# Leaving out the matmuls on zeros between the stages of a two-block transformer kernel

## The reference

```python
# first block, for each of two layers
a = rms_norm(h, norm_g[i, 0]); a = mixer_i(a, ...)
h = h + rms_norm(a, norm_g[i, 1])
f = conv_ffn(rms_norm(h, norm_g[i, 2]), ...)      # hidden width 2816
h = h + rms_norm(f, norm_g[i, 3])
# second block
h = h + 0.5 * swiglu(rms_norm_2(h, ffn1_norm), ...)   # hidden width 2752
h = h + hybrid_mixer(rms_norm_2(h, mix_norm), ...)
h = h + 0.5 * swiglu(rms_norm_2(h, ffn2_norm), ...)
out = rms_norm_2(h, final_norm)
```

## Time and profile before

| | us |
|---|---|
| median of the runs | 1247.5 |
| lowest, highest of three runs | 1238.12, 1247.79 |
| the profiled execution, its own time | 1248.45 |
| span of the profiled execution, first to last instruction | 1246.6 |
| TensorE busy (matmul) | 1195.6 |
| VectorE busy | 762.8 |
| ScalarE busy | 599.7 |
| GpSimd busy | 66.7 |

### The profile page before, as it was taken

One profiled execution on the slowest core, in us unless ns is written; L12 is line 12 of the kernel. 1 busy time (PEld: TensorE's weight loads), 2 busy tenths in 40 slices (PEclk: granted clock), 3 DMA queues, 4 the chain that ended last, 5 costly groups with the idle time before them and its releaser, 6 DMA issues.

```text
span 1246.6 us, 21628 instructions
## 1 busy us (share of the span) xinstructions
PE 1195.6 (96%) x8061; PEld 1068.2 (86%) x8075; DVE 762.8 (61%) x1066; ACT 599.7 (48%) x912; POOL 66.7 (5%) x93
## 2 busy tenths in 40 slices
PE   7999999999898989999999999999999999999997
PEld 6856999999698869999988999998887777999996
DVE  4854877776656558777767545546555556554554
ACT  5444554454555655545545443435554545443342
POOL 0201000000200010000001000001000210000000
PEclk9999999999999999999999999999998899999998
DMA  6404665666343347566655666653762014766661
GB/s 219 155 34 152 187 198 175 183 199 197 102 136 136 126 123 206 174 181 202 182 155 139 199 191 178 187 160 86 201 224 102 1 35 136 204 199 182 174 183 43
DMA packets 241059, 194.61 MB, mean 156 GB/s; under 512 B 11214, under 2 KB 223792, under 8 KB 241008
## 3 DMA queue, kind: packets, MB, share of 16 engines
q1 hardware_dynamic: 240928, 193.88, 51.8%
q10 hardware_dynamic: 80, 0.03, 0.0%
HBM read 192.84 MB, written 1.05 MB: 156 GB/s over the span
## 4 chain that ended last, share of the span: by engine, by line
PE 85%; DVE 7%; ACT 3%; DMA 2%; issue 1%; POOL 1%; SPq 0%; POOLq 0%; ACTq 0%; DVEq 0%
PE psum L572 25%; PE psum L573 25%; PE psum L574 25%; DVE lo_u L1629 1%; PE psum L1130 1%; DVE lo_u L1646 1%; ACT hi_u L1223 1%; DMA raw_u<-in_cmp_v_w 1%; PE psum L804 1%; PE psum L803 1%; PE psum L917 1%; DVE soft L1850 1%; PE psum L1087 1%; DMA raw_u<-in_mla_w_ukv 1%; DMA raw_u<-in_cmp_k_w 1%
## 5 line engine op out<-in xcount | busy, mean ns | idle before, releaser
L572 PE MATMUL psum<-act_hi,hi_u 128*128 128x256 f32 x1712 | 487.6, 285 | 7.8 <-DVE lo_u L1629 3.2
L574 PE MATMUL psum<-act_hi,lo_u 128*128 128x256 f32 x1712 | 484.9, 283 | 0.0
L573 PE MATMUL psum<-act_lo,hi_u 128*128 128x256 f32 x1712 | 484.8, 283 | 0.0
L1646 DVE TENSOR_TENSOR lo_u<-raw_u,hi_u 128x2048 fp32r<-128x2048 f32 (+3 forms) x122 | 273.7, 2243 | 244.5 <-ACT hi_u L1229 153.0
L572 PEld LDWEIGHTS psum<-act_hi,hi_u 128*128 128x128 f32 x1712 | 327.3, 191 | 16.2 <-issue 12.4
L573 PEld LDWEIGHTS psum<-act_lo,hi_u 128*128 128x128 f32 x1712 | 327.4, 191 | 3.3
L574 PEld LDWEIGHTS psum<-act_hi,lo_u 128*128 128x128 f32 x1712 | 327.4, 191 | 0.0
L1229 ACT ACTIVATE hi_u<-raw_u 128x2048 fp32r<-128x2048 f32 x72 | 137.7, 1912 | 88.6 <-PE psum L574 86.0
L572 PE MATMUL psum<-hi_d,hid_hi 128*128 128x512 f32 (+1 forms) x352 | 138.4, 393 | 1.4 <-DVE hid_lo L1736 1.4
L573 PE MATMUL psum<-lo_d,hid_hi 128*128 128x512 f32 (+1 forms) x352 | 138.0, 392 | 0.0
L574 PE MATMUL psum<-hi_d,hid_lo 128*128 128x512 f32 (+1 forms) x352 | 137.0, 389 | 0.0
(11 more groups left out here) (230 smaller groups left out, 1234.8 us busy)
## 6 DMA issues: line engine op xcount, KB each, us to landing
raw_u<-in_ffn_w_up SPq DMA_DIRECT2D x88, 512.0 KB, 5.5
raw_d<-in_ffn_w_down SPq DMA_DIRECT2D x86, 512.0 KB, 3.5
raw_u<-in_ffn_w_gu SPq DMA_DIRECT2D x84, 512.0 KB, 5.9
raw_u<-in_diff_w_qkv SPq DMA_DIRECT2D x24, 512.0 KB, 4.6
raw_u<-in_w_in SPq DMA_DIRECT2D x24, 512.0 KB, 4.0
raw_u<-in_mla_w_o SPq DMA_DIRECT2D x8, 512.0 KB, 3.7
raw_u<-in_diff_w_o SPq DMA_DIRECT2D x8, 512.0 KB, 3.7
raw_u<-in_w_out SPq DMA_DIRECT2D x8, 512.0 KB, 3.9
```

The source lines that it names most:

```text
L572: pe.matmul(o, s_hi, m_hi, start=start, stop=False)
L573: pe.matmul(o, s_hi, m_lo, start=False, stop=False)
L574: return pe.matmul(o, s_lo, m_hi, start=False, stop=stop)
L1646: dve.tensor_tensor(v[0], v[1], v[2].bitcast(F32), ALU.subtract).then_inc(S("lo_u_done"), 1)
```

## The change

The table's numbers all become zero, so that `keep_warm` issues nothing, and TensorE waits for `normed` and for `act_lo` without work.

```diff
-WARM = [(0, 0, 0)] + 4 * [(19, 3, 1)] + 2 * [(12, 3, 1)]
+WARM = 7 * [(0, 0, 0)]
```

## The result

The changed kernel takes 1247.41 us in the median of 20 runs (1245.17 to 1251.78), the kernel before 1241.58 us in the median of 20 runs next to them (1238.12 to 1247.79). The ratio is 1.0042 (95% interval 1.0028 to 1.0057), so the change costs 5.8 us in the medians, and by the interval 3.5 to 7.1. My forecast was 1255 us, 7.5 above the 1247.5 that I had as the median of before. The distance was near; the point from which I measured it was not.

A forecast was written before the change was run, and what follows sets the result against it. TensorE's time bounds the kernel; five places at 0.2 + 1.1 = 1.3 us make 6.5, the fourth adds 0.5, together 7.0; 1248.45 + 7.0 = 1255.5, in terms of the median 1254.5, stated as 1255 us, range 1247 to 1263.

The forecast's parts named there:

- What bounds the kernel: Whole kernel: TensorE, busy 96% of the span; work lost ahead of a feed-forward stage is not made good in it.
- The clock falls at all six places: Ahead of the six feed-forward stages: rests without zeros, five to six microseconds at the longest, bring the low clock.
- The transposes, 0.2 us a place: Transposes of `normed`: eight take 1.97 us at low clock, not 1.09; only part of the second eight's delay counts, 0.2 us.
- The real matmuls at the low clock, 2.5 us and 1.1 us of time: First 48 real matmuls of each stage: 2.5 us of them run at the low clock, costing 1.1 us.
- The bounds of 0 and 6.8: Real matmuls at low clock per place: from none to two short stretches, 6.8 us, costing 3.1.
- The fourth place, 0.5: Fourth feed-forward stage: real matmuls start 0.6 us sooner without low-clock zeros, then pay 1.1, so a cost of 0.5 us.
- The sum, 7.0: All six places: five at 1.3 us make 6.5, the fourth adds 0.5, together 7.0 us slower.
- the first (low clock far into the matmuls, from 4.1 us a place): First 48 matmuls of each stage: 3.4 to 6.8 us run low, 14.2 us in all, 1262.6 us; chance 0.22.
- That the clock comes back only under real matmuls: Six places: Trainium skill page's claim that transposes don't engage the full clock; the time would be the first rival's, 1262.6 us.
- The second, a stretch that goes away: Hybrid mixer: the changed kernel misses the long low-clock stretch, 7.0 - 6.2 leaves 1249 us; chance 0.13.
- the long stretch of the mixer: Hybrid mixer, 959.4 to 972.9 us in the profile before: 13.5 us at about half clock, priced at 6.2 us.
- The likeliest case, within 1% of before: Whole kernel: a time within about 1%, 12.5 us, of before, with chance 0.74.

The follow-up runs named there:

- the two guards: Changed kernel (no zeros at the six places) with zeros filling the waits in hybrid mixer and differential attention: 1245.05 us, ratio 1.0013 to the kernel before.
- the mixer's guard: Changed kernel plus eight matmuls on zeros in front of the hybrid mixer's wait: 1246.93 us, ratio 1.0025 to the kernel before.
- the transposes in place of zeros: Kernel before with each 512-column matmul on zeros replaced by two fp32 transposes of the identity of 128 columns: 1241.97 us, ratio 0.9999.
- only the first rest: Kernel before with only the first number of each place (19 and 12) set to zero, three and one zeros kept: 1249.68 us, ratio 1.004.
- the kernel before again: Kernel before, no edit, measured and profiled again: 1242.51 us, ratio 0.9988.

## Why the prediction was right or wrong

*What bounds the kernel*: right. The feed-forward stages have no idle time after the change either, and every delay at a place arrived at the end.

*The clock falls at all six places*: right in the trace of the changed kernel and in that with the two guards; with the mixer's guard alone it fell at five.

*The transposes, 0.2 us a place*: right. The first real matmul stands 9.90 us behind the last before it where it stood 9.65 (first and third place), 8.05 for 7.80 and 6.84 for 6.59 (fifth and sixth), and 0.01 later at the second.

*The real matmuls at the low clock, 2.5 us and 1.1 us of time*: right in the mean (2.4 us), from 0 to 4.1 in the single places. The bounds of 0 and 6.8 held all six. With the mixer's guard the five places that fell had 3.4 to 3.8, so 2.5 was a typical value, not a constant.

*The fourth place, 0.5*: wrong in sign, -0.57. The first part of it, 0.6 us gained because the low-clock zeros were out of the way, was exact; the 1.1 us behind it did not come, since the full clock was back at about 665.7 and the first real matmul started at 666.40. In the trace with the mixer's guard it was not back, and the place cost 1.07.

*The sum, 7.0*: near. The places add up to 6.4 us in the trace of the changed kernel, 7.7 and 4.3 in the two other traces without zeros. In the medians the change costs 5.8, and 7.5 between the two kernels that have the mixer's wait filled.

*The rivals*: the first (low clock far into the matmuls, from 4.1 us a place) was reached at one place of six and is out. That the clock comes back only under real matmuls is refuted by the transposes in place of zeros, and by the fourth place of the changed kernel, where it was back after the rest and sixteen transposes, 0.7 us before the first real matmul. The second, a stretch that goes away, is what happened: 7.0 - 6.2 is the arithmetic of the two profiled executions.

**The step that failed** is the one that set the sum on its base: "The profiled execution took 1248.45 us (span 1246.6), 0.95 above the median of the runs shown. 1248.45 + 7.0 = 1255.5". I had priced the long stretch of the mixer at 6.2 us from rows 12, and I had seen that the lowest run was 9.4 us under the median. Yet I treated the stretch as part of the kernel and its absence as a rival with a chance of 0.13. It is neither. Of the experiments' five traces in which that wait is unfilled, two have it and three have not. By my estimate near half of the executions of the kernel before have it (48 of 91 have a mean clock of 0.991 or less). None of the changed lines stands at that wait, and the profiled execution of the changed kernel was without it. What the runs showed in place of that base is a median of 1241.58 us. With it the same sum gives 1248.6, against 1247.41 measured. Of the error of 7.6 us the base has 5.9, the sum 1.2 (7.0 for 5.8), the rounding the rest.

The likeliest case, within 1% of before, is what was measured, and 1247.41 lies inside the range, 0.41 us above its lower edge. That is luck: the edge was set by rivals with small chances, not by a base that was 5.9 too high. Had I given the absence of the stretch the half that 1238.12 among three runs allowed, the centre would have stood near 1252 and the range would have begun at about 1244 (an estimate in hindsight).

What stays open: what decides, in one execution, whether the clock falls at a wait, and whether the change makes the mixer's stretch rarer. For the second speaks that filling that wait gave 3.5 us in the kernel before and 0.5 in the changed one, which would explain 5.8 us between the medians and 7.5 with the wait filled. The changed kernel's five runs over 1249.5 us are no sure sign of the stretch: their mean clocks are 0.972 to 0.975 where the others have 0.975 to 0.977, three of them too near for a stretch that lowers the mean by 0.005, and with that wait and the one in the differential attention filled there are still runs up to 1250.82. No profile of those five runs exists.

## What to carry to other kernels

When single low-clock stretches can be read in a profile, price each and ask which of them belong to the code and which to this execution, before setting a sum on that execution's time; three runs of which one lies 9 us lower are a warning that there are two groups. Matmuls on zeros paid here ahead of rests of 1.6 us and more, but only where a wait stood directly behind them: ten of them where none stood cost their full 2.0 us. The cheapest gain lay at a place the change did not touch, eight zeros in one wait of 1.6 us, worth 3.5 us in the median.

## What the runs showed of the hardware

- After the same wait the clock fell in one execution and not in the next. In the mixer 1.63 us led to 13.5 us of low clock in some executions (rows 12, and only the first rest) and to none in others (the changed kernel, the kernel before again). After 3.49 us at the end of the differential attention it fell in the changed kernel (447.3 to 450.6) and not with transposes in place of zeros. This is the wait there; its four transposes ran at the full pace, and the clock was 1.00 from 434 to 452 us:

```profile
441.43 0.66 PE L928 MATMUL psum<-ident,normed 128*128 128x128 f32 x4 [3.49 <-DVE normed L1877]
```

- Low clock can last while TensorE is never idle: 13.5 us busy of 13.5, in work of small matmuls, many of them with 64 rows or 15 columns, as this row of the timeline of before from that stretch:

```profile
960.51 1.03 PE L1084 MATMUL psum<-arena 64*128 64x15 f32 x4
```

- Real matmuls of 128 rows had the full clock back after 4.1 us of them at most in the places of the table. The longest that the traces have is 5.2 us (only the first rest, 445.2 to 450.4, 512 columns, without a gap).
- The float32 transposes of 128 columns hold the full clock up (four places with nothing else, clock 1.00), and it came back under them alone at two places and at the kernel's start.
- Short rests can be enough: at the first place, with 0.93 and 1.51 us around eight transposes, the clock fell in one trace; with 0.92 and 0.86 us and three zeros in the second rest it stayed up in all six traces that have the place so (in one of them with transposes for the zeros).
